# Hybrid decoder step: another order of the seven products of the first up-projection pair, and of the sums that they multiply

## The chip, the cores and the metric

The kernel runs on one core of one Trainium2 chip. The metric is the device time of one execution in microseconds; lower is better. In the views PE is TensorE (PEld its weight loads), DVE is VectorE, ACT is ScalarE, POOL is GpSimd and SP is SyncE.

## The reference, cut to what matters

One decoder step over 1,024 prompt tokens and 32 sample tokens: a combined projection, a gated DeltaNet group beside a differential-attention group, an output projection with a residual, and a gated MLP. The change lies at the start of the MLP. All the rest stays as it is.

```python
h = x + jnp.concatenate([o_g, o_d], axis=-1) @ w_out
hn = _rmsnorm(h, ffn_norm_g)
u, new_ffn = _causal_dwconv(hn @ w_up, ffn_buf, ffn_conv_w, ffn_conv_b)
y = h + (jax.nn.silu(u[..., :D_FF]) * u[..., D_FF:]) @ w_down
```

D_MODEL is 1,024, D_FF is 2,816, and w_up has 5,632 columns.

## The kernel before

`output_and_mlp` first makes `h` in 16 units of the output projection (8 blocks of 128 rows by two token halves of 528), then normalises it, then multiplies it by `w_up`. The normalised `h` lies in SBUF as `hT` (`feat` in the trace), 8 blocks by 1,056 tokens. `one` and `two` are its token halves; blocks j and HK + j (HK = 4) are the two halves of the model dimension.

The up projection is done in 22 pairs `p` of weight tiles (a gate tile and a value tile). Each pair is a two-by-two block product in Strassen's way (Winograd's form): seven products P1 to P7 instead of eight. Each takes a sum of weight blocks (S1 to S4 or plain blocks) and a sum of input blocks:

- P1 and P2 take the first half of tokens as it is (blocks j and HK + j of `one`); P3 takes blocks HK + j of `two`.
- P5 takes T1, P7 takes T3, P6 takes T2, P4 takes T4. T3 = x[HK+j, two] - x[j, two]; T2 = T3 + x[j, one]; T1 = x[j, two] - x[j, one]; T4 = x[HK+j, one] - T2.

The input operands are made once, in front of and during the first pair (p = 0). VectorE scales a block (`scale`, which reads a factor from PSUM), and makes T3 and T2 in place of block j (`token_sums(j)`, T3 over `two`, T2 over `one`). GpSimd makes T1 in a tile of its own, `m_t1` (`difference(j)`), and T4 in place (`last_sum(j)`). Since T2 overwrites x[j, one], `token_sums(j)` waits for T1 of the same j. Then each operand is split in two fp32r parts: ScalarE casts the high part (`x_high`), VectorE subtracts it from the source for the low part (`x_low`, two inputs in SBUF). A trio of products for one j (high by high, low by high, high by low) is six matmuls of 264 columns; a product has four j, so 24 matmuls.

The products of a pair share PSUM. P1 and P2 add up in pair tile 0, P6, P7 and P4 in tile 1, P5 and P3 in tile 2. Between additions the partial sums are copied out, so a product waits on the copy before it: P2 on `keep_u1` (ScalarE), P7 on `keep_u2`, P4 on `keep_u3`, P3 on `keep_22` (VectorE). In pair 0 each product also waits, for each j, on its low part.

Each engine runs its own queue in the order written. `ORDER0` is the order of the products on TensorE for pair 0; `turn` also takes from it which of the five weight slots a product uses and in which order ScalarE and VectorE split the weights (`up_high`, `up_low`). Pairs 1 to 21 go by `ORDER`. VectorE's queue in pair 0, from the second token half on, is: four `scale`; then `x_low("P5", j)`, `scale(1, HK + j)` and `token_sums(j - 1)` for each j; the low parts of P6 and P7; `keep_u2`; `up_low(5)`; the low parts of P4; `keep_u3`; `up_low(6)`; the low parts of P3; `keep_22`.

Of the kernel before, what the change touches and what calls it, by code (L numbers as in the profile page):

```python
# [24 lines left out]
KT = D // P  # L25
# [48 lines left out]
def r32(ap):  # L74

    return ap.bitcast(F32)
# [7 lines left out]
def samples(buf, start, pad, lo, n):  # L84

    return buf[:, start:start + NB * (pad + NL)].rearrange("p (b c) -> p b c", b=NB)[:, :, lo:lo + n]
# [2498 lines left out]
def output_and_mlp(nc, i, o, c, feat, o_hi, o_lo, o_at, feat_at, w_at, h_scratch, g_scratch, x_scratch, sem):  # L2585
# [3 lines left out]
    hT = feat[:, H:3 * H, :]  # L2589
# [5 lines left out]
    HK, HB = KT // 2, T // 2  # L2595
# [15 lines left out]
    t1 = m.at("m_t1", [P, HK, HB], F32, X_AT["P5"] + OPB // 2)  # L2611
# [24 lines left out]
    FIRST_IN = ("P1", "P6", "P5")  # L2636
    LAST_IN = ("P2", "P4", "P3")
    ORDER = ["P1", "P6", "P2", "P7", "P5", "P4", "P3"]
    ORDER0 = ["P1", "P2", "P5", "P6", "P7", "P4", "P3"]

    def order(p):
        return ORDER if p else ORDER0

# [11 lines left out]
    one, two = slice(0, HB), slice(HB, T)  # L2655
    halves = (one, two)

    def by_bank(ap):
        return ap.rearrange("p (x t) -> p x t", x=2)
# [37 lines left out]
    squared, gathered, scaled_h = sem("hn_squared"), sem("hn_gathered"), sem("hn_scaled")  # L2697
    t1_made, t3_made, t2_made, t4_made = (sem(f"m_{x}_made") for x in ("t1", "t3", "t2", "t4"))
# [50 lines left out]
    with nc.Block() as block:  # L2749
# [124 lines left out]
        @block.gpsimd  # L2874
        def _(pool):
            sub, add = ALU.subtract, ALU.add

            def last_sums(p):
                pool.wait_ge(sums_made, 4 * p + 2)
                if p:  # L2880
                    pool.wait_ge(up_lo, NP * p)
                nc.gpsimd.tensor_tensor(S1, A21, A22, add).then_inc(sums_made, 1)
                pool.wait_ge(sums_made, 4 * p + 3)
                nc.gpsimd.tensor_tensor(S4, A12, S2, sub).then_inc(sums_made, 1)

            def difference(j):
                pool.wait_ge(scaled_h, KT + j + 1)
                pool.wait_ge(unit_done, NO)
                nc.gpsimd.tensor_tensor(t1[:, j, :], hT[:, j, two], hT[:, j, one], sub).then_inc(t1_made, 1)

            def last_sum(j):
                pool.wait_ge(x_lo_done["P2"], j + 1)
                pool.wait_ge(t2_made, j + 1)
                nc.gpsimd.tensor_tensor(hT[:, HK + j, one], hT[:, HK + j, one], hT[:, j, one], sub).then_inc(t4_made, 1)

            def put_state(p, s):
                if p:
                    pool.wait_ge(taps, 2 * p - s)
                    pool.wait_ge(tail_kept, 2 * p - s)
                nc.gpsimd.tensor_copy(samples(pre[s], F_SAMPLE, F_PAD, 0, F_PAD),  # L2900
                                      col[:, s * FT + p, 0:NB * F_PAD].rearrange("p (b r) -> p b r", r=F_PAD)).then_inc(state_put, 1)

            def keep_tail(p, s):
                j = s * FT + p
                pool.wait_ge(kept, 5 * p + (3 if s else 5))
                nc.gpsimd.tensor_copy(tail[:, j, 0:F_PAD], pre[s][:, SEQ:SEQ + F_PAD])
                nc.gpsimd.tensor_copy(tail[:, j, F_PAD:F_TAIL].rearrange("p (b r) -> p b r", r=F_PAD),
                                      samples(pre[s], F_SAMPLE, F_PAD, NL, F_PAD)).then_inc(tail_kept, 1)

            last_sums(0)  # L2910
            for j in range(HK):
                difference(j)
            for j in range(HK):
                last_sum(j)
            for n in ("P3", "P4"):
                pool.wait_ge(x_lo_done[n], HK)
            for s in range(2):
                pool.memset(pre[s][:, 0:F_PAD], 0.0).then_inc(pads, 1)
            for p in range(FT):
                put_state(p, 1)  # L2920
                put_state(p, 0)
                keep_tail(p, 1)
                if p < LAST:
                    last_sums(p + 1)
                keep_tail(p, 0)

        @block.scalar
        def _(act):
# [25 lines left out]
            def x_high(name, j):  # L2954
                hi, lo = xop[name]
                if name in ("P1", "P2", "P3"):
                    n, x = (j if name == "P1" else HK + j), (1 if name == "P3" else 0)
                    act.wait_ge(scaled_h, KT * x + n + 1)
                    src = hT[:, n, halves[x]]
                    if name != "P3":  # L2960
                        act.wait_ge(o_lo_done, KT - 1)
                elif name == "P5":
                    act.wait_ge(t1_made, j + 1)
                    src = t1[:, j, :]
                elif name == "P4":
                    act.wait_ge(t4_made, j + 1)
                    src = hT[:, HK + j, one]
                else:
                    act.wait_ge(t2_made if name == "P6" else t3_made, j + 1)
                    src = hT[:, j, one if name == "P6" else two]  # L2970
                if name in ("P5", "P7", "P4", "P3"):
                    act.wait_ge(unit_done, NO)
                if name == "P6":
                    act.wait_ge(o_lo_done, KT - 1)
                nc.scalar.copy(hi[:, j, :], src).then_inc(x_hi_done[name], 1)
# [79 lines left out]

            keep_u1(0)
            for j in range(HK):
                x_high("P5", j)
            for j in range(HK):
                x_high("P6", j)  # L3060
            for j in range(HK):
                x_high("P7", j)
            nc.scalar.preload_act_table(ACT.Silu)
            up_high(5)
            for j in range(HK):
# [79 lines left out]
        def _(dve):  # L3145
            sub, add, mult = ALU.subtract, ALU.add, ALU.mult
# [43 lines left out]
            def scale(x, n):  # L3190
                dve.wait_ge(spread, x + 1)
                dve.wait_ge(h_out[KT * x + n], 16)
                h = by_bank(hT[:, n, halves[x]])
                nc.vector.scalar_tensor_tensor(out=h, in0=h, scalar=c["cols"][:, KT + n:KT + n + 1], in1=PW, op0=mult, op1=mult  # L3194
                                               ).then_inc(scaled_h, 1)

            def x_low(name, j):
                hi, lo = xop[name]
                dve.wait_ge(x_hi_done[name], j + 1)
                if name in ("P1", "P2", "P3"):  # L3200
                    src = hT[:, j if name == "P1" else HK + j, two if name == "P3" else one]
                elif name == "P5":
                    src = t1[:, j, :]
                elif name == "P4":
                    src = hT[:, HK + j, one]
                else:
                    src = hT[:, j, one if name == "P6" else two]
                nc.vector.tensor_tensor(lo[:, j, :], src, r32(hi[:, j, :]), sub).then_inc(x_lo_done[name], 1)  # L3208

            def token_sums(j):  # L3210
                dve.wait_ge(t1_made, j + 1)
                dve.wait_ge(scaled_h, KT + HK + j + 1)
                nc.vector.tensor_tensor(hT[:, j, two], hT[:, HK + j, two], hT[:, j, two], sub).then_inc(t3_made, 1)  # L3213
                dve.wait_ge(t3_made, j + 1)
                nc.vector.tensor_tensor(hT[:, j, one], hT[:, j, two], hT[:, j, one], add).then_inc(t2_made, 1)
# [12 lines left out]
            def up_low(s):  # L3228
                dve.wait_ge(up_hi, s + 1)
                hi, lo = wop[s % WR]  # L3230
                nc.vector.tensor_tensor(lo[:, :, :], W_OF[order(s // NP)[s % NP]], r32(hi[:, :, :]), sub).then_inc(up_lo, 1)  # L3231
# [29 lines left out]
            for n in range(HK):  # L3261
                scale(1, n)
            for j in range(HK):
                x_low("P5", j)
                scale(1, HK + j)
                if j:
                    token_sums(j - 1)
            token_sums(HK - 1)

            def plus(out, a, b):  # L3270
                return nc.vector.tensor_tensor(out, a, b, add)  # L3271
# [10 lines left out]
            def keep_u3(p):  # L3282
                dve.wait_ge(multiplied, turn(p, "P7") + 1)
                plus(by_bank(u3[:, :]), PY, by_bank(u1[:, :])).then_inc(kept, 1)
# [45 lines left out]
                                        samples(acc[1], F_SAMPLE, F_PAD, 0, NL), mult).then_inc(gated, 1)  # L3330

            for j in range(HK):
                x_low("P6", j)
            for j in range(HK):
                x_low("P7", j)
            keep_u2(0)
            up_low(5)
            for j in range(HK):
                x_low("P4", j)
            keep_u3(0)  # L3340
            up_low(6)
            for j in range(HK):
                x_low("P3", j)
            keep_22(0)
# [70 lines left out]
        def _(pe):  # L3415
# [103 lines left out]
            product(0, "P2", range(2, 4))  # L3519
            for name in ORDER0[2:]:  # L3520
                product(0, name)
# [101 lines left out]
```

## Time and profile before

| | us |
|---|---|
| median of 3 executions | 1628.84 (1628.6 to 1630.43) |
| the profiled execution | 1628.96 |
| its span in the trace | 1627.4 |
| TensorE busy in the span | 1515.5 (93%) |
| VectorE, ScalarE, GpSimd busy | 1054.6, 638.4, 395.5 |

The span is what the trace shows from its first to its last instruction. The profiled execution took 1.56 us more than its span. The first pair of the up projection begins at 880.40 us of the span, and its last product, P3, at 920.24 us. Rows of a timeline give start, duration, engine, line, operation and in brackets the idle time ahead of it with what ended it; several instructions alike in a row are merged and counted.

### The profile page before, as it was taken

What the parts mean: (1) busy time and instruction counts of PE and PEld (TensorE: products, weight loads), DVE (VectorE), ACT (ScalarE), POOL (GpSimd) and SP (SyncE); (2) the same over time, 40 slices, a digit from 0 to 9 for tenths busy, and PEclk for the clock granted to TensorE, in tenths of its full rate; (3) what the DMA queues carried; (4) which work ended last, traced back from release to release, by engine and by line L of the source; (5) the groups of instructions that cost most, each with busy time, mean ns of one, the idle gap of its engine ahead of it and who ended that gap; (6) DMA issues with size and microseconds to landing.
All of it is one profiled execution on the core that took longest, in us unless ns stands there. A gap on an engine that the chain in (4) does not pass through costs nothing.

```text
span 1627.4 us, 30132 instructions
## 1 busy us (share of the span) xinstructions
PE 1515.5 (93%) x11911; PEld 1430.0 (88%) x11911; DVE 1054.6 (65%) x1575; ACT 638.4 (39%) x1102; POOL 395.5 (24%) x750
## 2 busy tenths in 40 slices
PE   7999999898688888788999799999999999999998
PEld 6999999898577777644898799999999999999998
DVE  7444389777557676456547988887878787534420
ACT  6434242332334443353423444444444445423222
POOL 4000166554432243153002322222222220000000
PEclk8999999999789999899899799999999999999999
DMA  6211111232112311185542122222222226745333
GB/s 220 97 48 52 28 47 35 87 100 92 31 37 54 105 25 38 46 328 156 193 148 93 53 78 79 71 78 72 77 80 79 82 92 207 262 159 198 132 107 108
DMA packets 177981, 165.63 MB, mean 102 GB/s; under 512 B 24245, under 2 KB 157163, under 8 KB 176184
## 3 DMA queue, kind: packets, MB, share of 16 engines
q1 hardware_dynamic: 173528, 154.30, 30.7%
q0 software_dynamic: 1664, 6.29, 1.0%
q10 hardware_dynamic: 2656, 3.21, 0.5%
q8 instruction: 90, 1.47, 0.4%
q14 instruction: 43, 0.35, 0.1%
HBM read 125.68 MB, written 37.96 MB: 101 GB/s over the span
## 4 chain that ended last, share of the span: by engine, by line
PE 47%; DVE 2%; issue 1%; DMA 1%; ACT 1%; SPq 0%; POOL 0%; ACTq 0%; DVEq 0%; POOLq 0%
PE f_pair L3498 27%; PE f_pair L3544 15%; PE f_pair L3452 3%; DMA w_raw<-in_w_out 1%; DVE feat L3194 0%; PE f_pair L3578 0%; ACT w_hi L2936 0%; DVE m_xP_lo L3208 0%; DMA up_raw<-in_w_up 0%; DVE feat L3213 0%; SPq L2800 0%; PE f_pair L3512 0%; PE f_pair L3421 0%; DVE feat L3160 0%; DVE w_lo L3152 0%
## 5 line engine op out<-in xcount | busy, mean ns | idle before, releaser
L3498 PE MATMUL f_pair<-m_xP_hi,up_w_hi 128*128 128x264 f32 x1232 | 254.6, 288 | 12.8 <-DVE m_xP_lo L3208 9.4
L3498 PE MATMUL f_pair<-m_xP_lo,up_w_hi 128*128 128x264 f32 x1232 | 252.5, 286 | 0.0
L3498 PE MATMUL f_pair<-m_xP_hi,up_w_lo 128*128 128x264 f32 x1232 | 252.3, 286 | 0.0
L195 PE MATMUL proj<-x_hi,win_hi 128*128 128x352 f32 x672 | 220.1, 327 | 0.0
L195 PE MATMUL proj<-x_hi,win_lo 128*128 128x352 f32 x672 | 217.3, 323 | 0.0
L195 PE MATMUL proj<-x_lo,win_hi 128*128 128x352 f32 x672 | 216.9, 323 | 0.0
L3498 PEld LDWEIGHTS f_pair<-m_xP_hi,up_w_hi 128*128 128x128 f32 x1232 | 192.9, 190 | 15.3 <-issue 10.2
L3498 PEld LDWEIGHTS f_pair<-m_xP_lo,up_w_hi 128*128 128x128 f32 x1232 | 193.0, 190 | 0.0
L3498 PEld LDWEIGHTS f_pair<-m_xP_hi,up_w_lo 128*128 128x128 f32 x1232 | 192.5, 190 | 0.0
L3544 PE MATMUL f_pair<-dn_g_hi,dn_w_hi 128*128 128x352 f32 x528 | 171.9, 325 | 0.2 <-DVE f_pre L3271 0.2
L3544 PE MATMUL f_pair<-dn_g_lo,dn_w_hi 128*128 128x352 f32 x528 | 169.7, 321 | 0.0
L3544 PE MATMUL f_pair<-dn_g_hi,dn_w_lo 128*128 128x352 f32 x528 | 169.4, 321 | 0.0
L195 PEld LDWEIGHTS proj<-x_lo,win_hi 128*128 128x128 f32 x672 | 127.7, 190 | 0.0
L195 PEld LDWEIGHTS proj<-x_hi,win_hi 128*128 128x128 f32 x672 | 127.3, 189 | 0.3
L195 PEld LDWEIGHTS proj<-x_hi,win_lo 128*128 128x128 f32 x672 | 127.3, 189 | 0.0
L769 DVE RECIPROCAL head_root<-head_root 128x352 f32<-128x352 f32 x48 | 112.5, 2345 | 15.5 <-ACT head_root L591 15.3
L3319 DVE SCALAR_TENSOR_TENSOR f_acc<-f_pre,f_col,f_acc 128x1072 f32<-128x1072 f32 x88 | 116.8, 1329 | 0.0
L3355 DVE TENSOR_TENSOR dn_w_lo<-dn_raw,dn_w_hi 128x1024 fp32r<-128x1024 f32 x50 | 61.2, 1224 | 69.9 <-ACT dn_g_hi L3097 69.5
L3544 PEld LDWEIGHTS f_pair<-dn_g_lo,dn_w_hi 128*128 128x128 f32 x528 | 100.0, 189 | 0.0
L3544 PEld LDWEIGHTS f_pair<-dn_g_hi,dn_w_hi 128*128 128x128 f32 x528 | 99.0, 187 | 0.5 <-DVE f_pre L3271 0.5
L3231 DVE TENSOR_TENSOR up_w_lo<-up_sums,up_w_hi 128x512 fp32r<-128x512 f32 x88 | 72.0, 820 | 42.2 <-ACT up_w_hi L2990 42.2
L3544 PEld LDWEIGHTS f_pair<-dn_g_hi,dn_w_lo 128*128 128x128 f32 x528 | 99.1, 188 | 0.0
(462 smaller groups left out, 2932.3 us busy)
## 6 DMA issues: line engine op xcount, KB each, us to landing
dn_raw<-in_w_down SPq DMA_DIRECT2D x50, 512.0 KB, 4.0
up_raw<-in_w_up SPq DMA_DIRECT2D x44, 512.0 KB, 4.6
win_raw<-in_w_in SPq DMA_DIRECT2D x28, 512.0 KB, 3.9
g_scratch<-f_prod SPq DMA_DIRECT2D x22, 528.0 KB, 2.7
dn_g_in<-g_scratch SPq DMA_DIRECT2D x66, 176.0 KB, 3.6
p_key<-in_cache_k SPq DMA_DIRECT2D x32, 256.0 KB, 3.7
w_raw<-in_w_out SPq DMA_DIRECT2D x16, 512.0 KB, 6.1
x_scratch<-feat SPq DMA_DIRECT2D x1, 4224.0 KB, 12.0
```

Of the source, the lines that this page charges most:

```text
L195: mm = nc.tensor.matmul(out, w[:, k, :], x[:, k, g * TG:(g + 1) * TG], start=(k == 0 and i == 0), stop=(k == KT - 1 and i == 2))
L769: nc.vector.reciprocal(root[j % 2][:, :], root[j % 2][:, :]).then_inc(root_inverted, 1)
L3231: nc.vector.tensor_tensor(lo[:, :, :], W_OF[order(s // NP)[s % NP]], r32(hi[:, :, :]), sub).then_inc(up_lo, 1)
L3319: nc.vector.scalar_tensor_tensor(out=acc[s][:, 0:F_OUT], in0=pre[s][:, t:t + F_OUT], scalar=col[:, j, NB * F_PAD + t:NB * F_PAD + t + 1], ...
L3355: nc.vector.tensor_tensor(dw[s][1][:, 0, :], w_in[NTH_W[u] % NRAW][:, :], r32(dw[s][0][:, 0, :]), sub)
L3452: mm = nc.tensor.matmul(pair[s][:, b, 0:HQ], (w_hi, w_lo)[w][s][:, k, :], (o_hi, o_lo)[t][:, k, a:a + HQ], start=(k + x == 0), stop=(k == ...
L3498: mm = nc.tensor.matmul(pair[OF[name]][:, b, 0:HQ], w_[a][:, j, :], x_[t][:, j, b * HQ:(b + 1) * HQ], start=(name in FIRST_IN and j + x == ...
L3544: mm = nc.tensor.matmul(bank[f][:, 0:TG], w_[a][:, 0, f * P:(f + 1) * P], g_[t][:, 0, :], start=(k == KS[g][0] and x == 0), stop=(k == KS[ ...
```

## The change

TensorE's order in pair 0 is P1 P2 P6 P7 P5 P4 P3 instead of P1 P2 P5 P6 P7 P4 P3. On VectorE, T3 and T2 no longer wait for T1, and they stand ahead of the low parts of P6 rather than behind those of P5. On GpSimd, `difference(j)` now makes T1 as x[HK+j, two] - T2, and so waits for `scaled_h` of block HK + j and for `t2_made`; its four come ahead of the four `last_sum` as before. ScalarE casts P6, P7, P5 in place of P5, P6, P7. The low parts of P5 now stand behind `keep_u2` and `up_low(5)`; those of P4 behind `keep_u3` and `up_low(6)`, next to those of P3.

```diff
-    ORDER0 = ["P1", "P2", "P5", "P6", "P7", "P4", "P3"]
+    ORDER0 = ["P1", "P2", "P6", "P7", "P5", "P4", "P3"]
...
             def difference(j):
-                pool.wait_ge(scaled_h, KT + j + 1)
+                pool.wait_ge(scaled_h, KT + HK + j + 1)
+                pool.wait_ge(t2_made, j + 1)
                 pool.wait_ge(unit_done, NO)
-                nc.gpsimd.tensor_tensor(t1[:, j, :], hT[:, j, two], hT[:, j, one], sub).then_inc(t1_made, 1)
+                nc.gpsimd.tensor_tensor(t1[:, j, :], hT[:, HK + j, two], hT[:, j, one], sub).then_inc(t1_made, 1)
...
             for j in range(HK):
-                x_high("P5", j)
-            for j in range(HK):
                 x_high("P6", j)
             for j in range(HK):
                 x_high("P7", j)
+            for j in range(HK):
+                x_high("P5", j)
...
             def token_sums(j):
-                dve.wait_ge(t1_made, j + 1)
                 dve.wait_ge(scaled_h, KT + HK + j + 1)
...
             for j in range(HK):
-                x_low("P5", j)
                 scale(1, HK + j)
+                token_sums(j)
                 if j:
-                    token_sums(j - 1)
-            token_sums(HK - 1)
+                    x_low("P6", j - 1)
+            x_low("P6", HK - 1)
...
             for j in range(HK):
-                x_low("P6", j)
-            for j in range(HK):
                 x_low("P7", j)
             keep_u2(0)
             up_low(5)
             for j in range(HK):
-                x_low("P4", j)
+                x_low("P5", j)
             keep_u3(0)
             up_low(6)
+            for j in range(HK):
+                x_low("P4", j)
             for j in range(HK):
                 x_low("P3", j)
             keep_22(0)
```

VectorE's queue in pair 0, where the sums are made: SCALAR_TENSOR_TENSOR is `scale`, L3213 and L3215 make T3 and T2, L3208 is `x_low` (L3209 in the changed kernel, whose lines stand one lower there). Before:

```order
L3208 TENSOR_TENSOR m_xP5_lo_9823<-m_t1_9830,m_xP5_hi_9822 128x528
L3194 SCALAR_TENSOR_TENSOR feat_58<-feat_58,cols_51,f_pair3 128x528
L3213 TENSOR_TENSOR feat_58<-feat_58 128x528
L3215 TENSOR_TENSOR feat_58<-feat_58 128x528
L3213 TENSOR_TENSOR feat_58<-feat_58 128x528
L3215 TENSOR_TENSOR feat_58<-feat_58 128x528
L3208 TENSOR_TENSOR m_xP6_lo_9817<-feat_58,m_xP6_hi_9816 128x528 x4
L3208 TENSOR_TENSOR m_xP7_lo_9825<-feat_58,m_xP7_hi_9824 128x528 x4
L3271 TENSOR_TENSOR up_u1_9849<-f_pair1,up_u0_9848 128x528
L3231 TENSOR_TENSOR up_w0_lo_9835<-up_raw_9832,up_w0_hi_9834 128x512
L3208 TENSOR_TENSOR m_xP4_lo_9827<-feat_58,m_xP4_hi_9826 128x528 x4
L3271 TENSOR_TENSOR up_u2_9850<-f_pair1,up_u0_9848 128x528
```

These begin at the last low part of P5; L3271 is `keep_u2` and then `keep_u3`, L3231 is `up_low(5)`. The same place on VectorE in the changed kernel, from the last scaled block on:

```order
L3213 TENSOR_TENSOR feat_58<-feat_58 128x528
L3215 TENSOR_TENSOR feat_58<-feat_58 128x528
L3209 TENSOR_TENSOR m_xP6_lo_9817<-feat_58,m_xP6_hi_9816 128x528 x2
L3209 TENSOR_TENSOR m_xP7_lo_9825<-feat_58,m_xP7_hi_9824 128x528 x4
L3271 TENSOR_TENSOR up_u1_9849<-f_pair1,up_u0_9848 128x528
L3231 TENSOR_TENSOR up_w0_lo_9835<-up_raw_9832,up_w0_hi_9834 128x512
L3209 TENSOR_TENSOR m_xP5_lo_9823<-m_t1_9830,m_xP5_hi_9822 128x528 x4
L3271 TENSOR_TENSOR up_u2_9850<-f_pair1,up_u0_9848 128x528
L3231 TENSOR_TENSOR up_w1_lo_9837<-up_sums_9833,up_w1_hi_9836 128x512
L3209 TENSOR_TENSOR m_xP4_lo_9827<-feat_58,m_xP4_hi_9826 128x528 x4
L3209 TENSOR_TENSOR m_xP3_lo_9829<-feat_58,m_xP3_hi_9828 128x528 x4
```

Two low parts of P6 have moved up between the sums, those of P5 have moved down behind `keep_u2` and `up_low(5)`, and those of P4 behind `keep_u3`.

GpSimd's queue at the same place, in the changed kernel, has the same rows in the same order as before; only what the first row reads and waits for is another:

```order
L2882 TENSOR_TENSOR up_sums_9833<-up_raw_9832 128x512
L2884 TENSOR_TENSOR up_sums_9833<-up_raw_9832,up_sums_9833 128x512
L2890 TENSOR_TENSOR m_t1_9830<-feat_58 128x528 x4
L2895 TENSOR_TENSOR feat_58<-feat_58 128x528 x4
L2919 MEMSET f_pre0_9856 128x2
```

L2890 is `difference` and L2895 is `last_sum` (L2889 and L2894 before): the four T4 stand behind all four T1, and so now behind T2 of the last block.

## Rows read from the trace of the kernel before

**Rows 1.** The page, busy us of each engine (share of the span) and instructions.

```profile
PE 1515.5 (93%) x11911; PEld 1430.0 (88%) x11911; DVE 1054.6 (65%) x1575; ACT 638.4 (39%) x1102; POOL 395.5 (24%) x750
```

**Rows 2.** Waits of TensorE from 920 to 1360 us: total, times, longest.

```profile
PE f_pair L3498 <- issue: 0.9, 1, 0.9
```

**Rows 3.** Timeline of TensorE, 888 to 921 us: the products of pair 0.

```profile
888.88 0.40 PE L3498 MATMUL f_pair<-m_xP_hi,up_w_lo 128*128 128x264 f32 x2
892.00 0.78 PE L3498 MATMUL f_pair<-m_xP_hi,up_w_hi 128*128 128x264 f32 x2 [2.71 <-DVE m_xP_lo L3208]
...
905.36 0.78 PE L3498 MATMUL f_pair<-m_xP_hi,up_w_hi 128*128 128x264 f32 x2 [3.83 <-DVE m_xP_lo L3208]
...
907.01 0.81 PE L3498 MATMUL f_pair<-m_xP_hi,up_w_hi 128*128 128x264 f32 x2
...
910.70 0.64 PE L3498 MATMUL f_pair<-m_xP_hi,up_w_lo 128*128 128x264 f32 x2
912.18 0.49 PE L3498 MATMUL f_pair<-m_xP_hi,up_w_hi 128*128 128x264 f32 x2 [0.85 <-issue]
...
916.19 0.48 PE L3498 MATMUL f_pair<-m_xP_hi,up_w_hi 128*128 128x264 f32 x2 [0.85 <-issue]
...
920.24 0.48 PE L3498 MATMUL f_pair<-m_xP_hi,up_w_hi 128*128 128x264 f32 x2 [0.89 <-issue]
```

**Rows 4.** Timeline of VectorE, 887 to 921 us: scaling, sums, low parts, copies.

```profile
887.87 2.79 DVE L3194 SCALAR_TENSOR_TENSOR feat<-feat,cols,f_pair 128x528 f32<-128x528 f32 x4 [2.27 <-PE f_pair L3438]
...
892.45 1.14 DVE L3208 TENSOR_TENSOR m_xP_lo<-m_t,m_xP_hi 128x528 fp32r<-128x528 f32 x1
...
894.19 1.14 DVE L3213 TENSOR_TENSOR feat<-feat 128x528 f32<-128x528 f32 x1
895.36 0.71 DVE L3215 TENSOR_TENSOR feat<-feat 128x528 f32<-128x528 f32 x1
895.99 0.70 DVE L3208 TENSOR_TENSOR m_xP_lo<-m_t,m_xP_hi 128x528 fp32r<-128x528 f32 x1
...
902.91 1.69 DVE L3215 TENSOR_TENSOR feat<-feat 128x528 f32<-128x528 f32 x1
904.52 6.14 DVE L3208 TENSOR_TENSOR m_xP_lo<-feat,m_xP_hi 128x528 fp32r<-128x528 f32 x8
...
915.38 0.71 DVE L3271 TENSOR_TENSOR up_u<-f_pair,up_u 128x528 f32<-128x528 f32 x1 [0.23 <-PE f_pair L3498]
...
916.61 2.56 DVE L3208 TENSOR_TENSOR m_xP_lo<-feat,m_xP_hi 128x528 fp32r<-128x528 f32 x4
919.30 0.84 DVE L3271 TENSOR_TENSOR f_pre<-f_pair,up_u 128x264 f32<-128x264 f32 x3
```

**Rows 5.** GpSimd: line L2889 (min/median/max ns), then its timeline.

```profile
L2889 POOL TENSOR_TENSOR m_t<-feat x4: 1302/1546/1779, 888.7 to 893.0; 128x528 f32<-128x528 f32 x4
...
896.22 1.64 POOL L2894 TENSOR_TENSOR feat<-feat 128x528 f32<-128x528 f32 x1 [1.45 <-DVE feat L3215]
...
902.40 1.63 POOL L2894 TENSOR_TENSOR feat<-feat 128x528 f32<-128x528 f32 x1 [1.45 <-DVE feat L3215]
```

**Rows 6.** Timelines of VectorE and of GpSimd, 922 to 926 us, in pair 1.

```profile
922.75 1.24 DVE L3231 TENSOR_TENSOR up_w_lo<-up_sums,up_w_hi 128x512 fp32r<-128x512 f32 x1
923.91 1.78 DVE L3231 TENSOR_TENSOR up_w_lo<-up_raw,up_w_hi 128x512 fp32r<-128x512 f32 x1
...
923.51 1.62 POOL L2884 TENSOR_TENSOR up_sums<-up_raw,up_sums 128x512 f32<-128x512 f32 x1
```

**Rows 7.** One-microsecond windows: length, PE, PEld, DVE, ACT, POOL busy, granted clock, DMA.

```profile
429.00:430.00 1.00, 0.75 (x6) 0.75 (x8) 0.74 (x2) 0.35 (x3) 0.00 (x0) 0.50 0.00 0
434.00:435.00 1.00, 1.00 (x10) 0.88 (x9) 0.65 (x1) 0.23 (x1) 0.00 (x0) 0.98 0.00 0
891.00:892.00 1.00, 0.00 (x1) 0.03 (x1) 1.00 (x2) 0.63 (x1) 1.00 (x2) 0.71 0.00 0
911.00:912.00 1.00, 0.34 (x2) 0.03 (x1) 0.63 (x2) 1.00 (x3) 0.00 (x0) 0.55 0.00 0
```

## The prediction

> **What bounds the kernel now.** The page first: TensorE is busy for 93% of the span [rows 1], so only a place where it stands still or runs at half clock can give time. The wait table says that from 920 us on, through all the later pairs, it stands still for 0.9 us in all [rows 2]. What pair 0 gains or loses up to the start of its P3 (920.24 before) therefore reaches the end unchanged: nothing behind P3 has slack to take it up. So I compute one number, the new start of P3.
>
> TensorE's timeline shows the loss that the change is after. P2 ends at 889.1. P5 starts at 892.00, P6 at 905.36, P7 at 912.18, P4 at 916.19, P3 at 920.24 [rows 3]. At full clock a product of 12 trios takes about 2.9 us (12 pairs of matmuls at 0.243), four of them 11.7, and 31.1 us passed. The granted clock fell at 891.4 (0.71 of that microsecond) and came back at 911.9 (0.55) [rows 7]. Between them the level was 1.2 GHz.
>
> Then VectorE's timeline, since TensorE waited for low parts: from 887.87 to keep_22's end at 920.14 it has hardly a gap [rows 4]. Before P3 it must do a fixed set of work, the same in both kernels. So the most that reordering can give is small, and what counts is how long its instructions are held up and whether it now waits for TensorE.
>
> **What holds VectorE up.** A subtraction with both inputs in SBUF takes 0.70 us, as the one at 895.99 [rows 4]. While GpSimd works it takes 1.14 or 1.69. In detail: GpSimd's T4 ends at 904.03 (902.40 + 1.63) [rows 5], VectorE's T2 started at 902.91 ends at 904.60 [rows 4], 0.57 later. In pair 1 GpSimd ends at 925.13 and VectorE at 925.69, 0.56 later; before that VectorE's instruction had ended at 923.99, and GpSimd, issued at 923.51, ended 1.14 us behind it although VectorE's next instruction was issued at 923.91 [rows 6]. At 896 the same: VectorE ends at 896.69 [rows 4], GpSimd at 897.86 [rows 5], 1.17 later. So they alternate: after one ends, the other, already waiting, runs, 0.56 us for VectorE and 1.15 for GpSimd, 1.72 for a pair of them. The scaling, whose second input is in PSUM, isn't held up: four take 2.79 beside GpSimd [rows 4, 5].
>
> The Trainium skill says the same of the cause (SBUF — State Buffer, "Who interferes with whom"): the read interface is a lock held for the whole instruction, the later one blocks fully. The trace agrees, with its 0.57 us after GpSimd's end; the page's advice to schedule by what is off the critical path speaks against four T4 in a row beside the low parts. By bandwidth sharing instead of a lock, the sum below would be some 4 us less.
>
> **The change part by part.**
>
> 1. Until 887.87 nothing differs but which weight sum goes into slots 2 to 4: the same three casts and subtractions in a row. Cost 0.
>
> 2. T3 and T2 first. Four scalings end at 890.66, the fifth at 891.4; T3(0) and T2(0) with 0.03 us ahead of each end at 892.85. GpSimd starts 0.15 later (896.07 to 896.22 [rows 4, 5]), so T1(0) runs 893.0 to 894.3 (minimum 1.302 [rows 5]). T3(1) is held until 894.87, T2(1) ends at 895.6. From here a turn is low part of P6 (0.62), GpSimd's T1 behind it (1.17) with the scaling under it, T3 (0.56), T2 (0.74): 3.09 us. T2(2) ends at 898.7, T2(3) at 901.8, the low part P6(2) at 902.4. This is the old pace: T1 in place of T4 beside the sums.
>
> 3. The four T4. Before, three of them ran under the loop and the last beside P6's low parts, eight of which took 6.14 for 8 x 0.62 = 5.0 [rows 4]. Now they are queued behind T1(3), which waits for T2(3): it ends at 903.6, the low part P6(3) at 904.15. Then four T4 alternate with four low parts of P7: 4 x 1.72 = 6.9, so P7(3) ends at 911.05. keep_u2 stands behind it (0.68, PSUM input): 911.75. P7 starts on TensorE at 911.85. What is queued behind GpSimd's new wait is these four T4 and nothing that anyone needs sooner; ScalarE's casts of P4 need T4(3) (910.5) and are done at about 911.1, long before use.
>
> 4. TensorE meanwhile: P6(0) starts at about 896.3 instead of P5 at 892.00, its trios at 899.4, 902.5 and 904.2, all over at 905.8; then it stands still for 6 us. Before, P6 started at 905.36 and P7 at 912.18. So when P7 starts, P5 is not yet done, where it was before. P7 is at 911.85 only 0.33 us earlier, and at half clock: the clock has fallen (a shorter stop had made it fall at 891.4). P6 before had 9 trios in 4.33 us (907.01 to 911.34) at that level [rows 3], so 12 take 5.65. P7 ends at 917.5 if the clock stays low. It rose 6.5 us after work set in before (905.36 to 911.9) and 4.8 us after in another place (429.25 to 434.0) [rows 3, 7]; by 6.5 P7 is wholly at half clock, by 4.8 it ends at 917.2.
>
> 5. From P7's end to P3: before, keep_u3 starts 0.04 behind the product's end and takes 0.71 [rows 4]; up_low(6) ends at +1.35; eight low parts, P4's and P3's, follow at 0.62 = 4.96 (four in 2.56, first to last [rows 4]); from the last one's end (919.17) to P3's start (920.24) there are 1.07 us [rows 3, 4]. Together 7.38. VectorE has finished the low parts of P5 at 914.9 and waits 2.6 us for P7, since keep_u3 stands ahead of P4's low parts. P5 and P4 on TensorE take 5.8 and hide under the 7.38; P5 behind P7 does save the 0.85 us stop ahead of P4 at 916.19 [rows 3], which is then off the path. P3 starts at 917.5 + 7.38 = 924.9, or 924.6 by the shorter rise.
>
> The load of the next weights waits for up_low(5), which stands at 911.7 against 912.0: cost 0, ScalarE has slack for it until 925.
>
> **Sum.** 924.9 - 920.24 = +4.6, or +4.3 with the shorter rise. I take +4.3: the place at 434.0 began, as P7 will, with unbroken work, where P6 before had a stop ahead of 907.01. The profiled execution would take 1628.96 + 4.3 = 1633.3, the median 1628.84 + 4.3 = 1633.1.
>
> **The rivals.**
>
> A, as summed: +3.7 to +4.7, the end +3.7 if the clock comes back about 3.5 us into P7. For it: every hold in rows 4 to 6 fits one number. Chance 0.65.
>
> B, VectorE gets two turns for one of GpSimd's where both are queued, or the clock comes back sooner: two holds fewer are 2.3 us less, so +1.5 to +3.6. Against it: rows 6 show VectorE's instruction issued 0.08 us before its predecessor ended and still behind GpSimd. Chance 0.16.
>
> C, the clock stays low into P5 and P4: each takes 5.3 instead of 2.9, P4 ends at 928 and P3 waits for it, +8 at most. It decides only if the rise takes over 8.3 us of work. Chance 0.04.
>
> D, not slower: the low parts of P7 aren't held. Place: VectorE from 902 on. The holds of the loop (3 x 0.4), P6(3)'s 1.0 and P7's 4.4 go: P7's low parts end at about 904.3, keep_u2 at 905.0, P7 ends at 910.75 at half clock, P3 starts at 918.1: -2.1, 1626.7. It decides if those four take under 0.8 us each; then the change is no slower. Against it is the hold of 1.1 us in the eight low parts. With half of the holds: 0. Chance 0.10 for -2.1 to +0.5.
>
> E, the same with P7 at full clock, because TensorE's pauses become too short: P7 takes 3.2, and P3 starts at 915.7: -4.5, 1624.3. Chance 0.05.
>
> **How the numbers follow.** About 0.2% (3.3 us) is what a measurement of this kernel can tell from no change. Slower by more: A, C and some of B (0.03) = 0.72. Faster by more: E, 0.05. Within: 0.23. The range takes in A and B, with 0.2 us for the spread of a median: 1630.0 to 1634.5; D, E and C, 0.19, are left out.
>
> **What would show it.** In the changed profile: P6's first matmul near 896.3; four low parts of P7 of about 1.7 us each between 904 and 911, GpSimd's T4 between them; TensorE idle for some 6 us ahead of P7 near 911.9; the clock at half for most of P7; no gap ahead of P5 and P4; VectorE idle ahead of keep_u3; P3 near 924.6; the same 0.9 us or less of waits behind it. If P7's low parts are 0.7 us long, step 3 is wrong and D holds; if P7 takes 3.2 us, step 4 is; if P3 waits for P4 and not for keep_22, C; if later pairs have new waits, the first step is wrong.

## The result: 0.27% slower

The changed kernel takes 1632.09 us (median of 20 runs), the kernel before 1628.07 in the same runs. The ratio is 1.0027, with a 95% interval of 1.0016 to 1.0038, so +4.4 us (2.6 to 6.2); the two medians lie 4.0 apart. I had forecast +4.3, and 1633.1 for the median. Of the 1.0 us between that and 1632.09, 0.8 is the kernel before, which came to 1628.07 in 20 runs where the forecast had started from 1628.84 in three.

Single executions of one kernel lie several microseconds apart (1620.3 to 1631.7 before, 1626.6 to 1637.2 changed), and the profiled one of the changed kernel is one of the short ones: its span is 1625.3 us against 1627.4. The profile page shows it:

```profile
span 1625.3 us, 30128 instructions
PE 1508.2 (93%) x11911; PEld 1424.7 (88%) x11911; DVE 1056.7 (65%) x1575; ACT 638.2 (39%) x1102; POOL 396.3 (24%) x750
```

The spans must not be compared as they stand. The first scaling of the second token half, behind which the kernels differ, starts at 882.12 us here and at 887.87 before [rows 4], and at 884.88 in another profile of the kernel before: the stages ahead, which are the same, vary by more than the change is worth. So I compare two stretches inside one trace, both from that first scaling: to P3's first matmul, and to the first matmul of the down projection, behind all 22 pairs. In two profiles of the kernel before they were 32.37 and 32.35, and 470.23 and 470.22: there they repeat to 0.02 us. In the changed kernel they don't, as its second profile shows below.

TensorE's timeline of the changed kernel (start, duration, operation, idle time ahead and its releaser), which answers to rows 3:

```profile
883.13 0.40 PE L3498 MATMUL f_pair<-m_xP_hi,up_w_lo 128*128 128x264 f32 x2
890.59 0.78 PE L3498 MATMUL f_pair<-m_xP_hi,up_w_hi 128*128 128x264 f32 x2 [7.05 <-DVE m_xP_lo L3209]
...
899.48 0.64 PE L3498 MATMUL f_pair<-m_xP_hi,up_w_lo 128*128 128x264 f32 x2
906.02 0.78 PE L3498 MATMUL f_pair<-m_xP_hi,up_w_hi 128*128 128x264 f32 x2 [5.90 <-DVE up_u L3271]
...
909.67 0.40 PE L3498 MATMUL f_pair<-m_xP_hi,up_w_lo 128*128 128x264 f32 x2
...
916.24 0.40 PE L3498 MATMUL f_pair<-m_xP_hi,up_w_lo 128*128 128x264 f32 x2
918.16 0.48 PE L3498 MATMUL f_pair<-m_xP_hi,up_w_hi 128*128 128x264 f32 x2 [1.51 <-issue]
```

P7 begins at +23.90 from the first scaling (24.31 before), P3 at +36.04. TensorE stands still for 7.05 us behind P2 and 5.90 us ahead of P7, and runs P5 and P4 without a stop behind P7. The spacing of its matmuls shrinks from 0.44 to 0.24 at 909.67, 3.6 us into P7: the granted clock came back there. VectorE and GpSimd in the same stretch, answering to rows 4 and 5:

```profile
882.12 3.46 DVE L3195 SCALAR_TENSOR_TENSOR feat<-feat,cols,f_pair 128x528 f32<-128x528 f32 x5 [2.27 <-PE f_pair L3438]
...
895.94 9.36 DVE L3209 TENSOR_TENSOR m_xP_lo<-feat,m_xP_hi 128x528 fp32r<-128x528 f32 x6
905.22 0.69 DVE L3271 TENSOR_TENSOR up_u<-f_pair,up_u 128x528 f32<-128x528 f32 x1
...
910.83 0.71 DVE L3271 TENSOR_TENSOR up_u<-f_pair,up_u 128x528 f32<-128x528 f32 x1 [1.84 <-PE f_pair L3498]
...
912.05 5.03 DVE L3209 TENSOR_TENSOR m_xP_lo<-feat,m_xP_hi 128x528 fp32r<-128x528 f32 x8
917.22 0.84 DVE L3271 TENSOR_TENSOR f_pre<-f_pair,up_u 128x264 f32<-128x264 f32 x3
```

```profile
897.77 6.96 POOL L2895 TENSOR_TENSOR feat<-feat 128x528 f32<-128x528 f32 x4
```

Six low parts (P6(2), P6(3) and P7's four) take 9.36 us, while the eight at 912.05 take 5.03, 0.62 for each. The view of the line, from 897 to 905.5 us, gives the five held ones (min, median, max in ns):

```profile
L3209 DVE TENSOR_TENSOR m_xP_lo<-feat,m_xP_hi x5: 1655/1801/1819, 896.7 to 903.5; 128x528 fp32r<-128x528 f32 x5
```

GpSimd's four T4 lie between them, 1.74 us each. Behind P3 nothing is given back. TensorE's waits from 918 to 1360 us and its first matmul of the down projection (changed, then before):

```profile
PE f_pair L3498 <- issue: 1.5, 1, 1.5
PE f_pair L3544 <- DVE f_pre L3271: 0.2, 1, 0.2
```

```profile
1356.03 0.33 PE L3544 MATMUL f_pair<-dn_g_hi,dn_w_hi 128*128 128x352 f32 x1
```

```profile
1358.10 0.33 PE L3544 MATMUL f_pair<-dn_g_hi,dn_w_hi 128*128 128x352 f32 x1
```

The 1.5 us are the stop ahead of P3. 1356.03 - 882.12 = 473.91, and 1358.10 - 887.87 = 470.23: +3.68, the same as P3's +3.67.

### The profile page after: what moved, and what is told of

Same layout as the page of the kernel before. It is cut to its first block, busy times and chain, and to the rows that moved or that the text cites. A ratio compares the mean times of both kernels' runs of the same rounds, so it can differ in the third digit from the quotient of the medians.

```text
span 1625.3 us, 30128 instructions
## 1 busy us (share of the span) xinstructions
PE 1508.2 (93%) x11911; PEld 1424.7 (88%) x11911; DVE 1056.7 (65%) x1575; ACT 638.2 (39%) x1102; POOL 396.3 (24%) x750
## 4 chain that ended last, share of the span: by engine, by line
PE 48%; DVE 2%; DMA 1%; issue 1%; ACT 0%; SPq 0%; ACTq 0%; DVEq 0%
PE f_pair L3498 27%; PE f_pair L3544 16%; PE f_pair L3452 5%; DMA w_raw<-in_w_out 1%; DVE m_xP_lo L3209 1%; PE f_pair L3578 0%; DVE feat L3195 0%; DVE feat L3213 0%; SPq L2800 0%; PE f_pair L3512 0%; PE f_pair L3421 0%; ACT y_rows L3143 0%; DVE dn_w_lo L3355 0%; DVE up_w_lo L3231 0%; PE f_pair L3438 0%
## 5 line engine op out<-in xcount | busy, mean ns | idle before, releaser
L3231 DVE TENSOR_TENSOR up_w_lo<-up_sums,up_w_hi 128x512 fp32r<-128x512 f32 x88 | 72.0, 820 | 41.9 <-ACT up_w_hi L2991 41.8
```

## The experiments

All times in this table are microseconds from the first of the scalings. "Pair 0 from P3" is P3's first matmul, "down" the first matmul of the down projection. Differences in the last column are against 470.23.

| kernel | P7 | pair 0 from P3 | down | |
|---|---|---|---|---|
| before | 24.31 | 32.37 | 470.23 | |
| before, again | 24.30 | 32.35 | 470.22 | 0.0 |
| changed | 23.90 | 36.04 | 473.91 | +3.7 |
| changed, again | 23.88 | 36.68 | 474.55 | +4.3 |
| order_alone | 21.43 | 34.17 | 472.04 | +1.8 |
| t4_on_vector | 19.44 | 34.36 | 473.79 | +3.6 |
| t4_on_vector_2 | 19.43 | 32.94 | 472.36 | +2.1 |
| t4_behind_p7 | 19.43 | 33.88 | 473.28 | +3.1 |
| p4_low_first | 23.88 | 34.15 | 471.96 | +1.7 |
| warm_changed | 24.04 | 34.56 | 472.44 | +2.2 |
| changed_both | 24.04 | 34.25 | 472.12 | +1.9 |
| warm_before | 23.63 | 31.66 | 469.54 | -0.7 |
| before_t4_vec_warm | 20.6 | 31.11 | 470.50 | +0.3 |
| before_t4_vec_warm_2 | 20.6 | 31.12 | 469.03 | -1.2 |

**Repeats.**

> The kernel before once more, for the same stretch: it was 32.37; TensorE's P7 started at full clock there and VectorE set the pace, so 32.2 to 32.6, if the clock rises by the end of P6 again, and up to 34.6 if P7 also runs at half clock.

> The changed kernel once more, to see how far the stretch from the first scaling to P3 repeats. It was 36.04 in the profile. All of it but the rise of the clock within P7 is fixed by the program, so 35.9 to 36.9 by when the clock rises.

Before repeated to 0.02 us. The changed kernel came to 36.68: P7 again started at +23.88, but the clock rose later in it. One-microsecond windows of the first and the second profile, with the granted clock as the number behind the last bracket:

```profile
909.00:910.00 1.00, 1.00 (x7) 1.00 (x7) 0.00 (x0) 0.00 (x0) 0.00 (x0) 0.68 1.13 331
```

```profile
913.00:914.00 1.00, 1.00 (x8) 1.00 (x8) 0.10 (x1) 0.62 (x1) 0.00 (x0) 0.75 0.91 226
```

0.68 means that the clock was full for the last 0.36 us of the window, so it rose at 909.64, 3.6 us into P7 (906.02). 0.75 puts the rise at 913.5, 5.1 us into P7 (908.43 in that trace). P7 took 4.77 us in the one and 5.43 in the other, and that is the difference between the two profiles. Why the clock rises sooner or later in one and the same program was not found out.

**Is it GpSimd beside P7's low parts?** VectorE makes T4 behind the low parts of P5.

```diff
-            for j in range(HK):
-                last_sum(j)          # on GpSimd
...
                 x_low("P5", j)
+            for j in range(HK):
+                last_sum(j)          # on VectorE
             keep_u3(0)
```

> The changed kernel, with the four T4 made by VectorE behind the low parts of P5 instead of by GpSimd beside the low parts of P7. The measure is the stretch from the first of the four scalings to the first matmul of P3 (32.37 us before, 36.04 changed). My theory, alternation on a shared read interface: the four low parts of P7 shrink from about 1.7 us to 0.62 each, P7 starts some 4.4 us sooner, VectorE does 2.5 us more itself, and the stretch is 32.9 (32.3 to 33.5). Rival, the cost is the half clock and the product order alone: P7's low parts stay long or P7 is as late as before, and the stretch is 36 or, with VectorE's 2.5 us on top, up to 38.

The cause is right: six low parts now take 4.91 us instead of 9.36 (one of them is still held, by the last T1), and P7 starts at +19.44 instead of +23.90, 4.46 sooner. But P3 came at 34.36 and not at 32.9. VectorE's timeline shows why:

```profile
905.59 4.91 DVE L3202 TENSOR_TENSOR m_xP_lo<-feat,m_xP_hi 128x528 fp32r<-128x528 f32 x6
910.43 0.69 DVE L3269 TENSOR_TENSOR up_u<-f_pair,up_u 128x528 f32<-128x528 f32 x1
912.57 0.69 DVE L3229 TENSOR_TENSOR up_w_lo<-up_raw,up_w_hi 128x512 fp32r<-128x512 f32 x1 [1.45 <-ACT up_w_hi L2984]
```

It reaches up_low(5) so early that ScalarE's cast isn't there; ScalarE has just loaded its table:

```profile
910.62 1.28 ACT L3057 ACT_TABLE_LOAD   x1
911.92 0.62 ACT L2984 CAST up_w_hi<-up_raw 128x512 fp32r<-128x512 f32 x1
```

So the load, which no engine waited for in the two original kernels, became the next wait. Moving it tests that:

```diff
-            nc.scalar.preload_act_table(ACT.Silu)
             up_high(5)
...
                 x_high("P3", j)
+            nc.scalar.preload_act_table(ACT.Silu)
```

> The kernel with T4 on VectorE again, with ScalarE's load of its table moved from ahead of up_high(5) to behind the casts of P3. In the first one VectorE idled 1.45 us ahead of up_low(5) for that cast, and the stretch was 34.36. Theory: the idling goes, and the stretch is 32.9 to 33.2. Rival, the half clock in P7 sets the end: 34.3 still.

P3 came at 32.94, and in this trace up_low(5) has no wait ahead of it (up_low(6) still waits 0.6 us for its cast in both):

```profile
907.49 0.69 DVE L3229 TENSOR_TENSOR up_w_lo<-up_raw,up_w_hi 128x512 fp32r<-128x512 f32 x1
```

With T4 off GpSimd and the load out of the way P3 is 3.1 us sooner than in the changed kernel. Yet both kernels give back 1.5 us of it behind P3 (34.36 and 473.79: 439.4 between, where the changed kernel has 437.9). A window of the first one around P3 has the reason in its seventh column, the granted clock:

```profile
925.00:930.00 5.00, 3.86 (x19) 3.89 (x20) 4.77 (x10) 2.60 (x4) 3.48 (x8) 0.66 0.02 5
```

TensorE, ahead of VectorE here, had paused 1.50 us ahead of P4 and 2.09 us ahead of P3, and the clock fell to its lower level as P3 began: a mean of 0.66 over 5 us is 3.4 us at the lower level. In the second one it fell 1.4 us into P3, after a single pause of this size:

```profile
921.06 0.48 PE L3498 MATMUL f_pair<-m_xP_hi,up_w_hi 128*128 128x264 f32 x2 [2.10 <-issue]
...
922.72 0.65 PE L3498 MATMUL f_pair<-m_xP_hi,up_w_hi 128*128 128x264 f32 x2
```

**Only the time at which T4 runs.** GpSimd keeps T4, but starts it behind P7's low parts.

```diff
             def last_sum(j):
+                pool.wait_ge(x_lo_done["P7"], HK)
                 pool.wait_ge(x_lo_done["P2"], j + 1)
```

> The changed kernel, with one more wait: GpSimd's T4 wait until the low parts of P7 are made. They then run beside keep_u2, up_low(5) and the low parts of P5, where VectorE idles for 1.84 us later on. Theory: P7's low parts take 0.62 us each, P7 starts 4.4 us sooner, up_low(5) and three low parts of P5 are held by 1.1 us each instead, and the stretch is 33.9. Rival, P4's casts now come too late: 36 or more.

33.88, and P7 at 19.43. The hold has moved to where it was expected:

```profile
907.05 1.14 DVE L3232 TENSOR_TENSOR up_w_lo<-up_raw,up_w_hi 128x512 fp32r<-128x512 f32 x1 [1.45 <-ACT up_w_hi L2992]
908.12 4.80 DVE L3210 TENSOR_TENSOR m_xP_lo<-m_t,m_xP_hi 128x528 fp32r<-128x528 f32 x4
```

The low parts of P5 take 4.80 instead of 2.55. The sum behind the expected 33.9 had no 1.45 us wait for the cast in it, and it had four holds of 1.1 us where 2.7 us came (0.46 on up_low(5), 2.25 on P5's low parts), since T4 had begun in that wait. So its agreement to 0.02 us is in part luck. Here too TensorE paused ahead of P3 (2.10 us), the clock fell in P3, and 1.5 us were given back behind it: 473.28.

**The order without the new T1.** The new order and queues, but T1 made from x[j, two] - x[j, one], ahead of T3 and T2.

```diff
             def difference(j):
-                pool.wait_ge(scaled_h, KT + HK + j + 1)
-                pool.wait_ge(t2_made, j + 1)
+                pool.wait_ge(scaled_h, KT + j + 1)
...
             def token_sums(j):
+                dve.wait_ge(t1_made, j + 1)
```

> The new order of products and queues, but T1 made as in the kernel before, from the two unsummed halves, with T3 and T2 waiting for it. Then the T1 run beside the scalings and the T4 beside the loop, and the low parts of P7 are free. Theory: the start of the loop is held by T1 (about 2 us), P7's low parts take 2.5 instead of 6.9 us, P7 starts at about +21.5, and the stretch is 33.6 to 34.6, between 32.37 and 36.04. Rival, GpSimd's instructions cost the same wherever they stand: 36.

34.17, and +1.8 to the down projection. The clock rose 5.0 us into P7 here, as in the second profile of the changed kernel, whose loss was +4.3; so some 1.8 of it are with the order and 2.5 with T1's new place. Against the first profile (+3.7) it is half and half. GpSimd, then VectorE:

```profile
887.03 5.54 POOL L2889 TENSOR_TENSOR m_t<-feat 128x528 f32<-128x528 f32 x4 [6.55 <-DVE feat L3194]
```

```profile
889.76 1.66 DVE L3213 TENSOR_TENSOR feat<-feat 128x528 f32<-128x528 f32 x1
891.45 1.68 DVE L3215 TENSOR_TENSOR feat<-feat 128x528 f32<-128x528 f32 x1
...
901.99 4.92 DVE L3208 TENSOR_TENSOR m_xP_lo<-feat,m_xP_hi 128x528 fp32r<-128x528 f32 x6
```

T1's four start beside the scalings, which costs the scalings nothing (five in 3.46 us, as in the changed kernel, where GpSimd stood still beside them), and hold the first T3 and T2 (1.66 and 1.68 instead of 0.70), 2 us; P7's low parts are free. up_low(5) waited 1.44 us for its cast here too, but VectorE then waited 0.91 us for P7 all the same, so that this cost nothing.

**P4's low parts ahead of keep_u3.**

```diff
             for j in range(HK):
                 x_low("P5", j)
-            keep_u3(0)
-            up_low(6)
             for j in range(HK):
                 x_low("P4", j)
+            keep_u3(0)
+            up_low(6)
```

> The changed kernel, with the low parts of P4 put ahead of keep_u3 on VectorE. Theory: VectorE's 1.84 us of idling ahead of keep_u3 is filled, and the stretch from the first scaling to P3 goes from 36.04 to 34.2. Rival: keep_u3 comes later and P4 waits for it on TensorE so that nothing is won: 35.5 to 36.0.

34.15, 1.9 us less than in the first profile. VectorE has no wait left: behind P5's low parts `keep_u3` had waited for P7 with eight low parts queued behind it. The clock has a part in it. It rose 3.2 us into P7 in this trace, sooner than in either profile of the changed kernel, and TensorE ran from P7 to P3 without a stop, so that each tenth that P7 takes longer would have put P3 back by a tenth. P7 took 4.58 us here; with 4.77 or 5.43 P3 would stand at 34.3 or 35.0 (an estimate from these three traces), 1.7 us ahead of the changed kernel with the same P7. So the position of the copy is worth some 1.7 us, and the expected 34.2 was met with luck.

**The clock alone.** Extra matmuls in TensorE's waits, whose results are thrown away.

```diff
+            def warm(n, out, w):
+                for x in range(n):
+                    nc.tensor.matmul(out[:, x % 2, 0:HQ], wop[w][0][:, 0, :], xop["P1"][0][:, 0, 0:HQ], start=True, stop=True,
+                                     skip_group_check=True)
...
+            warm(52, pair[2], 3)
+            for j, n in enumerate((16, 16, 6, 50)):
+                product(0, "P6", range(j, j + 1))
+                warm(n, pair[2], 3)
```

> The changed kernel, with extra matmuls (operands of P1, results thrown away in the PSUM tile that P5 starts afresh) in TensorE's waits of the first pair: 52 behind P2, 16, 16 and 6 between the parts of P6, 50 behind P6. They change nothing but how busy TensorE is. Theory: the granted clock stays at full, P7 takes 3.2 us instead of 4.8, and the stretch goes from 36.04 to 34.4; P7 still starts at +23.9. Rival, P3 is set by VectorE's queue and not by P7: 36.0.

> The kernel before, with extra matmuls in TensorE's waits of the first pair (18 behind P2; 4, 16, 16 and 34 behind the parts of P5; 4 behind the first part and 14 behind the last part of P6). Theory: the clock stays at full, but P7 can start only when VectorE has made the low parts of P6 and P7 and keep_u2, so the stretch from the first scaling to P3 shrinks by 0.8 us at most, from 32.37 to 31.6, where the same in the changed kernel gives 1.6. Rival, the half clock costs both kernels the same: 30.8.

> The changed kernel with both single remedies: low parts of P4 ahead of keep_u3 (34.1 alone) and the extra matmuls (34.56 alone). Theory: both fill the same idling of VectorE ahead of keep_u3, after which VectorE's queue sets P3, so they don't add: 34.1. Rival, the savings are of different waits and add: 32.6.

In the changed kernel P7 starts at nearly the same time (24.04 against 23.90) and P3 comes at 34.56, 1.5 us sooner than in the first profile and 2.1 than in the second; in the kernel before it is 0.71. The granted clock of warm_changed over the whole stretch is full (seventh column):

```profile
886.00:925.00 39.00, 35.75 (x284) 34.57 (x284) 38.18 (x49) 17.40 (x29) 17.40 (x16) 1.00 0.10 28
```

So half clock is worth 1.5 to 2.1 us in the changed kernel and 0.7 before. The two remedies together gave 34.25, no better than P4's low parts first alone (34.15). With the extra matmuls alone VectorE waits 0.22 us ahead of keep_u3 instead of 1.84, so that P4's low parts first had little left to fill, and the two don't add.

**Both findings in the kernel before.** T4 on VectorE behind up_low(5), with the old order of products and extra matmuls (18; 4, 16, 13, 24 in and behind P5; 14 behind P6), and then 9 and 16 more ahead of P4 and P3.

```diff
             keep_u2(0)
             up_low(5)
+            for j in range(HK):
+                last_sum(j)          # on VectorE
+            keep_u3(0)
             for j in range(HK):
                 x_low("P4", j)
-            keep_u3(0)
```

> The kernel before (its own order of products) with the four T4 made by VectorE behind up_low(5), and with extra matmuls in TensorE's waits of the first pair. Theory: without T4 on GpSimd the sums and low parts of the loop are no longer held (3.2 us of holds go, 2.5 us of own work come), the clock stays at full, and the stretch from the first scaling to P3 goes from 32.37 to 30.9, below the 31.66 of the extra matmuls alone: 0.09% of the time, which five rounds will hardly tell. Rival, T4 costs VectorE as much when it makes it itself: 31.7 or more.

> The kernel before with T4 on VectorE and extra matmuls, now also 9 ahead of P4 and 16 ahead of P3. Without these the stretch from the first scaling to P3 was 31.11, but TensorE paused 1.51 and 2.67 us, the clock fell as P3 ran, and the stretch to the first matmul of the down projection was 470.5, against 470.23 in the kernel before. Theory: the clock stays up and the gain of 1.26 us arrives: 469.0 to the down projection, P3 at 31.1. Rival, the extra matmuls delay P4 and P3 or the clock falls all the same: 470.0 or more. In time it is 0.08%, too little to be told in five rounds.

The first came to 31.11 at P3, where 30.9 was expected, and to 470.50 at the down projection: 1.26 us won and 1.5 lost again. Its timeline of TensorE, and a window around P3:

```profile
913.33 0.48 PE L3498 MATMUL f_pair<-m_xP_hi,up_w_hi 128*128 128x264 f32 x2 [1.51 <-DVE m_xP_lo L3201]
919.18 0.50 PE L3498 MATMUL f_pair<-m_xP_hi,up_w_hi 128*128 128x264 f32 x2 [2.67 <-DVE f_pre L3269]
```

```profile
918.00:923.00 5.00, 3.82 (x19) 3.85 (x20) 4.76 (x10) 2.56 (x4) 3.45 (x8) 0.66 0.01 5
```

The second closed these two pauses, the clock stayed full, and the gain arrived: 469.03, 1.2 us below the kernel before. Of these, 0.7 are what the extra matmuls gave alone (warm_before, 469.54), and 0.5 came with T4 on VectorE. Five rounds give 1625.55 against 1627.87 us, ratio 0.9990 (0.9978 to 1.0003); the first gave 0.9997 (0.9981 to 1.0013). Neither is told apart from the kernel before by its time; by the stretch in one profile, the second is faster than both kernels.

## Why the prediction was right

The way, the mechanism and the size were right, and most steps came within a tenth of a microsecond; that the size came so close is luck in part (4). From the first scaling, forecast and measured in the first profile:

| step | forecast | measured |
|---|---|---|
| P6's first matmul | 8.4 | 8.47 |
| P7's low parts, one each | 1.72 | 1.74 |
| P7's first matmul | 23.98 | 23.90 |
| P7's end | 29.3 to 29.6 | 28.67, then 29.31 |
| from P7's end to P3 | 7.38 | 7.37 |
| P3 | 36.7 to 37.0 | 36.04, then 36.68 |

(Where the working of step 4, and the line on 11.7 us, say 12 or 9 trios, pairs of matmuls are meant: a product has four trios, or 12 pairs.)

1. *Nothing behind P3 has slack*: held. +3.67 at P3 is +3.68 at the down projection. The kernels made in the experiments show its limit: where TensorE paused for 2.09 to 2.67 us ahead of P3, the clock fell for 3.4 us in and behind P3, and 1.5 us were lost that P3's start doesn't show. A stop of 1.51 us there, as the changed kernel has, did not bring it down.

2. *The pace of the loop is the old one*: held, 3.10 us from one part of P6 to the next.

3. *T4 and the low parts of P7 alternate*: held. It rests on t4_on_vector, where taking T4 off GpSimd brings P7 forward by 4.46 us.

4. *P7 at half clock*: held, and the rise of the clock within it was mis-sized for the first profile. I took the rise 4.8 us into P7 or later; it came 3.6 us in in one profile and 5.1 in the other, so P7's end was 0.7 early in the first. That is the 0.6 us by which the forecast +4.3 is off there; the second profile has +4.3. The reason that I gave for 4.8 rather than 6.5, unbroken work, is not shown: under unbroken work the rise came 3.2, 3.6 and 5.1 us into the same P7 in three traces. In both profiles of the kernel before it came 6.5 us after the start of P6. That the forecast hit the second profile to a tenth is luck; +3.7 was as near at hand.

5. *VectorE waits for P7 ahead of keep_u3*: held (1.84 us instead of 2.6, for the same 0.7), and shown by p4_low_first, where it is gone.

"The new load of weights costs 0" held as well. What the prediction left out is ScalarE's table load. It cost nothing here, but it was the next limit, and the first expectation for t4_on_vector failed on it.

Rivals D and E (no holds) fall with the low parts of 1.66 to 1.82 us, C (clock low into P5) with the rise inside P7. B's quicker rise is where the first profile leans, by 0.6 us. The upper end of the range, 1634.5, is 0.8 more than its terms give (1628.84 + 4.7 + 0.2 = 1633.7); the measured median lies inside either way.

The median's +4.4 us (2.6 to 6.2) and the stretches' +3.7 and +4.3 agree. But the interval of the medians is so wide that it tells only that the change is slower; the size rests on the stretches. Why the stages ahead of the scaling vary by up to 10 us between traces was not tried. The granted clock varies in them: from 500 to 780 us its mean is 0.95 where the scaling starts soonest (882.12) and 0.92 where it starts latest (891.78); that this is the cause is not shown.

## What to carry to other kernels

Work on an idle engine isn't free if it holds up the engine that sets the pace. Here four subtractions on GpSimd, beside VectorE's subtractions with both inputs in SBUF, put P7 off by 4.46 us, and VectorE makes them itself in 2.56. Put such work beside instructions that read PSUM, as the scalings here, which were not held, or count each one's full price. Where the holds were fewer, as in the kernel before, the same move was worth only 0.5 us. When one order of work is exchanged for another, follow the pacing engine's queue to the first copy that waits for the other engine, and look at what stands behind it. And judge by a stretch inside the trace that ends behind a point where both kernels do the same, not by the end of the edited part: a TensorE that stood still may pay later at the lower clock.

## What the runs showed of the hardware that I had not expected

Short pauses of TensorE can bring the clock down. A single one of 2.10 us ahead of P3 did in t4_on_vector_2, and pauses of 1.51 and 2.67 us, some 3 us of work apart, did in before_t4_vec_warm, where filling them to 0.42 and 0.75 us kept it up. A single one of 1.51 us in the changed kernel did not. In the long wait behind P2 it fell 2.2 us behind the last matmul in the first profile of either kernel (before: 891.4), but 3.7 us behind it in the second profile of the changed one and 5.2 us in p4_low_first, though the work ahead of it is the same. Extra matmuls of 264 columns in the waits kept 2.4 GHz through a stretch of 39 us where the changed kernel's four waits up to P7 come to 15.7 us.

GpSimd and VectorE alternated in every stretch shown here in which both had their next instruction waiting, and neither got two turns in a row. The Trainium skill (SBUF — State Buffer, "Who interferes with whom") has the lock and the full blocking. The trace of order_alone agrees: GpSimd's last T1 ends at 892.57, and the T2 that VectorE had issued at 891.45 ends at 893.13, 0.56 us later.
